# Dealing the products of the unit behind each gate unit out among the gate products, in the second layer of a four-layer model on one core

## The chip, the cores and the metric

One core of a Trainium2 chip runs the whole model in one launch. The metric is the device time of one execution in microseconds, and smaller is better. "Time before" is the median of three runs.

## What is computed

The model has four layers over 512 positions of width 1024: an even mixer (convolution and pooling), an odd mixer (a gated linear recurrence), an S5 state-space layer and a windowed attention layer, the last two with MLPs. The change is in the second layer, the odd mixer:

```python
def odd_mixer(h, w_in, conv_w, conv_b, w_rg, b_rg, w_ig, b_ig, lam, w_out):
    p = h @ w_in                                  # 1024 -> 2 x 1536
    xr, gate = jnp.split(p, [W_LRU], axis=-1)     # 12 heads of 128 each
    xc = causal_depthwise_conv(xr, conv_w, conv_b)
    xh = xc.reshape(bsz, t, LRU_HEADS, LRU_HD)
    r = sigmoid(einsum("bthi,hij->bthj", xh, w_rg) + b_rg)
    i = sigmoid(einsum("bthi,hij->bthj", xh, w_ig) + b_ig)
    log_a = -LRU_C * r * softplus(-lam)
    a = exp(log_a)
    bterm = sqrt(-expm1(2.0 * log_a)) * (i * xc)
    hs = associative_scan(a, bterm)               # over the positions
    y = hs * silu(gate)
    return y @ w_out
```

## The kernel before

**Units.** All matrix work is cut into 281 units in a fixed order (`ORDER`). A unit is a block of weights of 128 x 1024, that is eight 128x128 tiles. Products are made in float32 by splitting both operands in an upper part of reduced precision and the rest: wh x xh, wh x xl and wl x xh. So a unit is 24 matmuls of 512 columns on TensorE (PE). The helper `linear` (lines 310 on; its `product` is L315) runs a unit of one output block: it takes a PSUM bank, waits until that bank is free and the weights' upper part is there, runs sixteen matmuls with the upper weights, waits for the lower weights and runs the last eight.

**Weights.** SyncE (SP) loads unit i into one of three RAW buffers (`fetch`, L268) once the lower part of unit i-3 is made. ScalarE (ACT) makes the upper part WH (`high`, L287; it waits for the load and for the end of unit i-3 on PE, since there are three WH buffers), and GpSimd (POOL) the lower part WL (`low`, L291). Each engine has its own queue in program order; `highs(act, end)` and `lows(pool, end)` put in all roundings up to unit end-1 that are not in yet.

**The order of the second layer** is written out by hand (`ODD`): X0 X1 X2 X3 X4 **R0** X5 ... X11 **R1** G0 ... G5 **R2** G6 ... G11 O0 ... O7 Q0 ... Q3. X is a head's share of xr, G a head's share of the gate, R the two gate matrices of four heads, O and Q the output. Unit R has, for each of its four heads, a product for r and one for i (`mm3`, three matmuls each, lines L298 to L300). These use two PSUM banks of their own in turn (`rbanks`); a gate's bank is freed by ACT's sigmoid, which reads it (`act_gates`: L960 for r into GT, L965 for i into IX). The other units take four banks in turn (`banks`). The bank of an X is free when DVE has written the lower half of the convolved head (`split_lo`, L428, Yl), that of a G when DVE has written the lower half of y (L428 too).

**ACT's queue at an R** (`act_odd`): sigmoids of the first two heads; upper half of an earlier head (`split_hi`, L424, Yh); where the unit before was an X, the first tap of its convolution (L944); sigmoids of the other two heads; where the unit before was a G, its SiLU (L948); rounding of the weights of the unit two behind R (`highs(act, IDX[what] + 3)`); another upper half; rounding of the unit three behind; then tanh for four heads (L927), square root for four (L904) and exponentials (L993), two at once.

**DVE behind it:** for each head three operations on these (`lru_input`, L1072 to L1077) and the scan along the positions (L1082), between them the taps of the convolutions (L1016), the scaled outputs of the units (L421), the products of y (L1021) and the lower halves (L428). Behind R2 DVE also makes a block of coefficients for the third layer (`dve_b`, twice L1255, L1256, L1258: two products of a broadcast row and a table in SBUF, and their sum or difference). POOL multiplies the square root with the head (L1093), makes 1 - x of the tanh product (L1110) and adds the halves of the heads (L1105), between its roundings.

The change touches `pe_odd` and `act_odd`, and adds two functions on PE.

Of the kernel before, what the change touches and what calls it, by code (L numbers as in the profile page):

```python
# [32 lines left out]
for _n, _c in VECS:  # L33
# [15 lines left out]
ODD = ("X0 X1 X2 X3 X4 R0 X5 X6 X7 X8 X9 X10 X11 R1 G0 G1 G2 G3 G4 G5 R2 G6 G7 G8 G9 G10 G11 "  # L49
       "O0 O1 O2 O3 O4 O5 O6 O7 Q0 Q1 Q2 Q3").split()  # L50
EVEN = [(x[0], int(x[1:])) for x in EVEN]
ODD = [(x[0], int(x[1:])) for x in ODD]
# [46 lines left out]
class Signals:  # L99
# [12 lines left out]
    def inc(self, name, key, by=1):  # L112
        s = self.sem(name)
        self.count[name] += by
        assert (name, key) not in self.value, (name, key)
        self.value[name, key] = self.count[name]
        return s, by

    def at(self, name, key):
        s = self.sem(name)  # L120
        assert self.known is None or (name, key) in self.known, (name, key)
        return s, self.known[name, key] if self.known else 1
# [20 lines left out]
def program(nc, ctx, known, D):  # L143
# [128 lines left out]
    def highs(act, end):  # L272

        while upto["hi"] < min(end, len(ORDER)):
            high(act, upto["hi"])
            upto["hi"] += 1
# [17 lines left out]
    def weights(i):  # L294
        return WH[:, i % NS, :], WL[:, i % NS, :]
# [6 lines left out]
    def linear(pe, what, xh, xl, chunks, freed_by, ready=None, between={}, first=False):  # L302


        i = IDX[what]
        wh, wl = weights(i)
        b, before = banks.take(what, freed_by)
        if before:
            pe.wait_ge(*at(*before))
        pe.wait_ge(*at("w_hi" if first or not ready else "w_lo", i))  # L310
        chunks = list(chunks)
        ws = {c: slice(n * 128, n * 128 + 128) for n, c in enumerate(chunks)}

        def product(w, x, c, start=False, stop=False):
            return pe.matmul(b[:, :], w[:, ws[c]], x[:, c, :], start=start, stop=stop)  # L315

        for n, c in enumerate(chunks):
            if ready:
                pe.wait_ge(*at("x_hi", (ready, c)))
            product(wh, xh, c, start=n == 0)  # L320
            if first:
                pe.matmul(CB[0][:, 0:128], MEAN[:, :], MEAN[:, :], start=True, stop=True)
                if n:
                    pe.wait_ge(*at("x_lo", (ready, chunks[n - 1])))
                    product(wh, xl, chunks[n - 1])
            elif ready:
                product(wl, xh, c)
            else:
                product(wh, xl, c)
            if n in between:  # L330
                between[n]()
        if first:
            pe.wait_ge(*at("x_lo", (ready, chunks[-1])))
            product(wh, xl, chunks[-1])
        if first or not ready:
            pe.wait_ge(*at("w_lo", i))
        for c in chunks:
            if ready and not first:
                pe.wait_ge(*at("x_lo", (ready, c)))
                last = product(wh, xl, c, stop=c == chunks[-1])  # L340
            else:
                last = product(wl, xh, c, stop=c == chunks[-1])
        last.then_inc(*inc("unit", what))
# [449 lines left out]
    def odd_what(n):  # L793
        return ODD_UNIT[ODD[n][0]](ODD[n][1])

    rbanks = Banks([])
    rbanks.bank = banks.bank

    def pe_odd(pe):
        for _ in range(2):  # L800
            rbanks.queue.append(banks.queue.popleft())
        for n, (kind, c) in enumerate(ODD):
            what = odd_what(n)
            i = IDX[what]
            wh, wl = weights(i)
            if kind in "XG":
                linear(pe, what, P0h, P0l, range(8), ("x_lo", ("xc" if kind == "X" else "y", c)), "odd" if n == 0 else None)
            elif kind == "O":
                if c == 0:
                    banks.queue.extend(rbanks.queue)  # L810
                linear(pe, what, Yh, Yl, range(8), "h", "y" if c == 0 else None)
            elif kind == "R":
                pe.wait_ge(*at("w_lo", i))
                for h in range(4 * c, 4 * c + 4):
                    pe.wait_ge(*at("x_lo", ("xc", h)))
                    for j, r in enumerate("ri"):
                        b, before = rbanks.take((r, h), "evac_a")
                        pe.wait_ge(*at(*before))
                        ws = slice((h % 4) * 256 + 128 * j, (h % 4) * 256 + 128 * j + 128)
                        last = mm3(pe, b[:, :], wh[:, ws], wl[:, ws], Yh[:, h, :], Yl[:, h, :], True, True)  # L820
                        last.then_inc(*inc("unit", what if (h % 4, j) == (3, 1) else (r, h)))
            else:
                if c == 0:
                    for b in CB:
                        banks.add(b, ("turns", (7, 2)))
                elif c > 1:
                    pe_square_sums(pe, (2 * c - 4, 2 * c - 3))
                pe.wait_ge(*at("w_lo", i))
                for j in range(2):
                    b, before = banks.take(("q4", 2 * c + j), "h")  # L830
                    pe.wait_ge(*at(*before))
                    for kc in range(4):
                        if n == len(ODD) - 4 and j == 0:
                            pe.wait_ge(*at("x_lo", ("y", 8 + kc)))
                        ws = slice((4 * j + kc) * 128, (4 * j + kc) * 128 + 128)
                        last = mm3(pe, b[:, :], wh[:, ws], wl[:, ws], Yh[:, 8 + kc, :], Yl[:, 8 + kc, :], kc == 0, kc == 3)
                    last.then_inc(*inc("unit", what if j else ("q4", 2 * c)))
                    if (c, j) == (3, 0):
                        pe_square_sums(pe, (4, 5))
            if (kind, c) == ("X", 0):  # L840
                stat_sums(pe, "odd", pool=rbanks)
            elif (kind, c) == ("X", 1):
                stat_spread(pe, "odd", pool=rbanks)
# [17 lines left out]
    def kind_at(n):  # L861
        return ODD[n][0] if 0 <= n < len(ODD) else ""
# [20 lines left out]
    def pair(r, second):  # L883
        return [4 * r + 2 * second, 4 * r + 2 * second + 1]
# [5 lines left out]
    def act_odd(act):  # L890
        for n in range(len(ODD) + 3):
            for s, i in late(n):
                act_last(act, i, s)
            if n >= len(ODD):
                continue
            kind, c = ODD[n]
            what = odd_what(n)
            for r, d in gates_at(n):
                if d == 1:
                    for h in pair(r, 0) + pair(r, 1):  # L900
                        act.wait_ge(*at("lru_tanh", h))
                        if h > 3:
                            act.wait_ge(*at("lru_r", h - 4))
                        act.activation(lru_s(h), lru_t(h), ACT.Sqrt).then_inc(*inc("lru_sqrt", h))  # L904
                if d in (1, 3):
                    for h in pair(r, d == 3):
                        lru_exp(act, h)
            if kind == "R":
                act_gates(act, pair(c, 0))
                act_parts(act, n - 1)  # L910
                if kind_at(n - 1) == "X":
                    act_first(act, n - 1)
                act_gates(act, pair(c, 1))
                if kind_at(n - 1) == "G":
                    act_first(act, n - 1)
                highs(act, IDX[what] + 3)
                act_parts(act, n)
                highs(act, IDX[what] + 4)
            elif kind_at(n + 1) != "R":
                highs(act, min(IDX[what] + 4, GLU0))  # L920
                act_first(act, n)
            if kind == "R":
                for h in pair(c, 0) + pair(c, 1):
                    act.wait_ge(*at("evac_a", ("r", h)))
                    if h > 3:
                        act.wait_ge(*at("scan", h - 4))
                    act.activation(lru_t(h), GT[:, h % 4, :], ACT.Tanh, scale=SP4[:, 0, h:h + 1]).then_inc(*inc("lru_tanh", h))  # L927
            elif kind_at(n + 1) != "R":
                act_parts(act, n)
            if kind in "OQ":  # L930
                act_last(act, n, 0)
            elif (kind, c) in (("X", 2), ("X", 9), ("G", 5)):

                act.activation(SM[:, 12 + c % 2:13 + c % 2], SM2[:, 0:1], ACT.Sigmoid)
# [1937 lines left out]
```

## Time and profile before

| what | us |
|---|---|
| median of three runs | 1722.12 |
| lowest and highest of the three | 1722.08, 1727.5 |
| the profiled execution, its own time | 1726.02 |
| the profiled execution, its span | 1724.1 |
| second layer from R0 to the last gate unit (timeline) | 363.5 to 493 |

How to read it: the page gives for each engine the time in which it was busy. A matmul's record lasts about 390 ns, but matmuls are pipelined and follow each other in less; the time of one is that of many back to back. Line numbers are those of the kernel. In a timeline row the square brackets hold the idle time of that engine just before the instruction and the instruction that released it; a wait for several things is put down to the one that came last by the profile.

### The profile page before, as it was taken

Reading aid. Unit: us, or ns where it says so; the run is one execution under the profiler, and the core shown is the slowest. Engines: PE = TensorE matmul, PEld = TensorE weight load, DVE = VectorE, ACT = ScalarE, POOL = GpSimd, SP = SyncE. Lnnn points to the kernel's source line nnn. Section 1 sums busy time; section 2 is a strip of 40 time slices with the busy share of each in tenths; the row PEclk is TensorE's granted clock in tenths of the full one; section 3 lists DMA queues with packets and bytes.
Section 4 is the critical chain, followed back from the end, with each engine's and each line's share of the span. In section 5 each row is a group of like instructions: output and inputs, shape, how many; then the busy total and the mean of one; then the engine's idle time right before and its main releaser. Section 6 shows DMA issues by size and latency. Waiting matters only on the chain.

```text
span 1724.1 us, 20954 instructions
## 1 busy us (share of the span) xinstructions
PE 1698.1 (98%) x8056; PEld 1399.4 (81%) x8056; DVE 869.5 (50%) x1250; ACT 763.1 (44%) x1203; POOL 969.2 (56%) x606
## 2 busy tenths in 40 slices
PE   9999999999999999999999999999999999999998
PEld 7888888777778898888888888887678888888887
DVE  3999997757787785522212121485644221212124
ACT  5333335476867763343222223443664332323234
POOL 5858755657678575654444445664556444444464
PEclk9999999999999999999999999999999999999999
DMA  4322323222245234222222222222112222222221
GB/s 168 106 99 86 111 97 123 90 73 95 86 181 195 67 124 134 98 98 98 98 95 94 95 97 98 89 95 98 38 50 99 98 96 94 95 96 97 98 98 61
DMA packets 56258, 172.65 MB, mean 100 GB/s; under 512 B 6496, under 2 KB 14816, under 8 KB 55264
## 3 DMA queue, kind: packets, MB, share of 16 engines
q1 hardware_dynamic: 56160, 171.33, 28.7%
q8 instruction: 64, 1.05, 0.2%
q14 instruction: 34, 0.28, 0.0%
HBM read 165.01 MB, written 6.29 MB: 99 GB/s over the span
## 4 chain that ended last, share of the span: by engine, by line
PE 68%; DVE 6%; ACT 3%; issue 2%; POOL 2%; DMA 1%; SPq 0%; DVEq 0%; ACTq 0%; POOLq 0%
PE B L315 57%; PE B L2439 1%; PE B L2441 1%; PE B L2437 1%; PE B L2314 1%; PE B L2235 1%; PE B L2335 1%; PE B L298 1%; DVE SW L1150 1%; DVE B L1016 1%; PE B L300 1%; PE B L299 1%; PE B L2411 0%; PE B L2405 0%; PE B L2407 0%
## 5 line engine op out<-in xcount | busy, mean ns | idle before, releaser
L291 POOL TENSOR_TENSOR WL<-RAW,WH 128x1024 fp32r<-128x1024 f32 x281 | 681.5, 2427 | 610.0 <-ACT WH L287 609.7
L287 ACT ACTIVATE WH<-RAW 128x1024 fp32r<-128x1024 f32 x281 | 296.7, 1058 | 627.3 <-PE B L315 595.5
L315 PE MATMUL B<-P0h,WH 128*128 128x512 f32 x1096 | 428.6, 391 | 4.1 <-ACT WH L287 2.3
L315 PE MATMUL B<-P0l,WH 128*128 128x512 f32 x1096 | 422.2, 390 | 0.4 <-DVE P0l L432 0.3
L315 PE MATMUL B<-P0h,WL 128*128 128x512 f32 x1096 | 276.4, 389 | 0.0
L315 PEld LDWEIGHTS B<-P0h,WH 128*128 128x128 f32 x1096 | 206.0, 188 | 48.8 <-DVE Yl L428 2.6
L315 PEld LDWEIGHTS B<-P0l,WH 128*128 128x128 f32 x1096 | 206.0, 188 | 43.2 <-DVE P0l L432 1.1
L315 PEld LDWEIGHTS B<-P0h,WL 128*128 128x128 f32 x1096 | 205.7, 188 | 42.8
L439 DVE TENSOR_TENSOR H<-H,B 128x512 f32<-128x512 f32 x88 | 60.2, 686 | 288.2 <-PE B L315 288.1
L315 PE MATMUL B<-P1h,WH 128*128 128x512 f32 x448 | 174.7, 390 | 0.0
L1967 DVE SCALAR_TENSOR_TENSOR TMP<-B,RS 128x512 f32<-128x512 f32 x64 | 44.1, 691 | 258.4 <-PE B L315 244.1
L315 PE MATMUL B<-P1l,WH 128*128 128x512 f32 x448 | 169.8, 389 | 0.0
L611 DVE SCALAR_TENSOR_TENSOR B<-UP,VE,B 128x512 f32<-128x512 f32 x232 | 156.5, 751 | 1.6 <-ACT B L550 1.6
L315 PE MATMUL B<-P1h,WL 128*128 128x512 f32 x448 | 115.2, 389 | 0.0
L315 PEld LDWEIGHTS B<-P1h,WL 128*128 128x128 f32 x448 | 84.1, 188 | 17.5
L315 PEld LDWEIGHTS B<-P1l,WH 128*128 128x128 f32 x448 | 84.1, 188 | 17.4
L315 PEld LDWEIGHTS B<-P1h,WH 128*128 128x128 f32 x448 | 84.1, 188 | 17.4
L368 POOL TENSOR_TENSOR ACC<-ACC,TMP 128x512 f32<-128x512 f32 x54 | 78.1, 1447 | 22.2 <-ACT TMP L359 21.4
L315 PE MATMUL B<-P2h,WH 128*128 128x512 f32 x144 | 56.2, 391 | 0.7 <-ACT P2h L424 0.7
L2298 POOL TENSOR_SCALAR TMP<-TMP,AS 128x256 f32<-128x256 f32 (+1 forms) x64 | 28.7, 468 | 43.8 <-DVE AS L2292 43.8
L432 DVE SCALAR_TENSOR_TENSOR P0l<-H,VE,P0h 128x512 fp32r<-128x512 f32 x40 | 48.5, 1228 | 9.1 <-ACT P0h L424 9.1
L315 PE MATMUL B<-P2l,WH 128*128 128x512 f32 x144 | 52.6, 389 | 0.0
(354 smaller groups left out, 2699.5 us busy)
## 6 DMA issues: line engine op xcount, KB each, us to landing
RAW<-in_w SPq DMA_DIRECT2D x281, 512.0 KB, 3.2
PX<-in_zeros SPq DMA_DIRECT2D x4, 1024.0 KB, 9.8
H<-in_xT SPq DMA_DIRECT2D x8, 256.0 KB, 5.3
U<-u SPq DMA_DIRECT2D x32, 64.0 KB, 2.0
g<-GB SPq DMA_DIRECT2D x8, 256.0 KB, 2.2
GB<-g SPq DMA_DIRECT2D x32, 64.0 KB, 2.0
out<-Q SPq DMA_DIRECT2D x4, 512.0 KB, 3.6
CA<-in_zeros SPq DMA_DIRECT2D x1, 1920.0 KB, 10.0
```

The lines of the kernel that those rows point to most:

```text
L287: act.activation(WH[:, i % NS, :], RAW[:, i % NR, :], ACT.Copy).then_inc(*inc("w_hi", i))
L291: pool.tensor_tensor(WL[:, i % NS, :], RAW[:, i % NR, :], WH[:, i % NS, :].bitcast(F32), ALU.subtract).then_inc(*inc("w_lo", i))
L298: pe.matmul(out, wh, xh, start=start, stop=False)
L299: pe.matmul(out, wl, xh, start=False, stop=False)
L300: return pe.matmul(out, wh, xl, start=False, stop=stop)
L315: return pe.matmul(b[:, :], w[:, ws[c]], x[:, c, :], start=start, stop=stop)
L368: pool.tensor_tensor(ACC[:, :], ACC[:, :], tmp(c % 2), ALU.add).then_inc(*inc("acc", (k, c)))
L432: dve.scalar_tensor_tensor(dst, src, g, hi.bitcast(F32), ALU.mult, ALU.subtract).then_inc(*inc("x_lo", (k, c)))
L439: dve.tensor_tensor(H[:, n, :], H[:, n, :], banks.bank[what][:, :], ALU.add).then_inc(*inc("h", key))
L611: dve.scalar_tensor_tensor(chunk(c) if j == 30 else CB[c % 2][:, :], UP[:, c, j:j + T], w, CB[c % 2][:, :], ALU.mult, ALU.add).then_inc(*i ...
L1967: dve.scalar_tensor_tensor(mlp_tmp(q, c), banks.bank[what][:, :], 0.0, rs(f"mlp{l}"), ALU.max, ALU.mult).then_inc(*inc("evac_d", what))
L2298: pool.tensor_scalar(s_head(n, h), s_head(n, h), st[:, 16 + h:17 + h], 1.0, ALU.mult, ALU.mult).then_inc(*inc("att_w", (n, h)))
```

## The change

On PE a unit X or G that directly follows an R is no longer run by `linear`. Its 24 matmuls come from a generator, `pe_beside`: the same matmuls in the same order with the same waits on the bank, the upper and the lower weights. `pe_odd` takes two of them after each of the eight gate products of R (sixteen in all) and the last eight behind the last gate. The units concerned are X5 behind R0, G0 behind R1 and G6 behind R2. On ACT, the rounding of the weights of the unit two behind R moves from behind the sigmoids to the front of R's part of the queue.

```diff
--- before.py
+++ after.py
@@ -796,6 +796,29 @@
     rbanks = Banks([])
     rbanks.bank = banks.bank
 
+    def pe_beside(pe, what, freed_by):
+
+        i = IDX[what]
+        wh, wl = weights(i)
+        b, before = banks.take(what, freed_by)
+        pe.wait_ge(*at(*before))
+        pe.wait_ge(*at("w_hi", i))
+        for c in range(8):
+            ws = slice(128 * c, 128 * c + 128)
+            pe.matmul(b[:, :], wh[:, ws], P0h[:, c, :], start=c == 0, stop=False)
+            yield
+            pe.matmul(b[:, :], wh[:, ws], P0l[:, c, :], start=False, stop=False)
+            yield
+        pe.wait_ge(*at("w_lo", i))
+        for c in range(8):
+            last = pe.matmul(b[:, :], wl[:, 128 * c:128 * c + 128], P0h[:, c, :], start=False, stop=c == 7)
+            if c == 7:
+                last.then_inc(*inc("unit", what))
+            yield
+
+    def odd_bank_free(kind, c):
+        return "x_lo", ("xc" if kind == "X" else "y", c)
+
     def pe_odd(pe):
         for _ in range(2):
             rbanks.queue.append(banks.queue.popleft())
@@ -803,14 +826,17 @@
             what = odd_what(n)
             i = IDX[what]
             wh, wl = weights(i)
-            if kind in "XG":
-                linear(pe, what, P0h, P0l, range(8), ("x_lo", ("xc" if kind == "X" else "y", c)), "odd" if n == 0 else None)
+            if kind in "XG" and kind_at(n - 1) == "R":
+                pass
+            elif kind in "XG":
+                linear(pe, what, P0h, P0l, range(8), odd_bank_free(kind, c), "odd" if n == 0 else None)
             elif kind == "O":
                 if c == 0:
                     banks.queue.extend(rbanks.queue)
                 linear(pe, what, Yh, Yl, range(8), "h", "y" if c == 0 else None)
             elif kind == "R":
                 pe.wait_ge(*at("w_lo", i))
+                beside = pe_beside(pe, odd_what(n + 1), odd_bank_free(*ODD[n + 1]))
                 for h in range(4 * c, 4 * c + 4):
                     pe.wait_ge(*at("x_lo", ("xc", h)))
                     for j, r in enumerate("ri"):
@@ -819,6 +845,10 @@
                         ws = slice((h % 4) * 256 + 128 * j, (h % 4) * 256 + 128 * j + 128)
                         last = mm3(pe, b[:, :], wh[:, ws], wl[:, ws], Yh[:, h, :], Yl[:, h, :], True, True)
                         last.then_inc(*inc("unit", what if (h % 4, j) == (3, 1) else (r, h)))
+                        for _ in range(2):
+                            next(beside)
+                for _ in beside:
+                    pass
             else:
                 if c == 0:
                     for b in CB:
@@ -906,6 +936,7 @@
                     for h in pair(r, d == 3):
                         lru_exp(act, h)
             if kind == "R":
+                highs(act, IDX[what] + 3)
                 act_gates(act, pair(c, 0))
                 act_parts(act, n - 1)
                 if kind_at(n - 1) == "X":
@@ -913,7 +944,6 @@
                 act_gates(act, pair(c, 1))
                 if kind_at(n - 1) == "G":
                     act_first(act, n - 1)
-                highs(act, IDX[what] + 3)
                 act_parts(act, n)
                 highs(act, IDX[what] + 4)
             elif kind_at(n + 1) != "R":
```

## Rows read from the trace of the kernel before

**Rows 1.** The page, part 1: busy time of each engine.

```profile
PE 1698.1 (98%) x8056; PEld 1399.4 (81%) x8056; DVE 869.5 (50%) x1250; ACT 763.1 (44%) x1203; POOL 969.2 (56%) x606
```

**Rows 2.** Busy time by stretch: us, busy (instructions) per engine, clock, DMA share, GB/s.

```profile
363.50:371.00 7.50, 6.30 (x26) 4.32 (x25) 5.70 (x8) 5.63 (x9) 0.07 (x1) 1.00 0.19 65
...
409.80:419.30 9.50, 6.26 (x26) 4.28 (x25) 7.96 (x12) 7.08 (x12) 3.62 (x2) 1.00 0.18 55
419.30:451.90 32.60, 32.60 (x145) 27.02 (x144) 21.51 (x31) 28.43 (x38) 27.82 (x18) 1.00 0.29 101
451.90:458.70 6.80, 6.26 (x25) 4.23 (x24) 1.99 (x3) 5.22 (x9) 0.00 (x0) 1.00 0.14 57
```

**Rows 3.** The chain that ended last: start, us, what.

```profile
347.31 16.36 PE B L315 x72
```

**Rows 4.** Timeline, PE and ACT, around R0: start, us, engine, line, operation [idle <-releaser].

```profile
363.52 0.39 PE L298 MATMUL B<-Yh,WH 128*128 128x512 f32 x1
...
364.40 0.69 ACT L960 ACTIVATE GT<-B,VE 128x512 f32<-128x512 f32 x1 [2.49 <-PE B L300]
...
365.23 0.47 PE L298 MATMUL B<-Yh,WH 128*128 128x512 f32 x1 [0.19 <-ACT GT L960]
...
371.15 0.69 ACT L965 ACTIVATE IX<-B,VE 128x512 f32<-128x512 f32 x1
...
371.74 1.05 ACT L287 ACTIVATE WH<-RAW 128x1024 fp32r<-128x1024 f32 x1
...
372.68 0.59 ACT L424 ACTIVATE Yh<-B 128x512 fp32r<-128x512 f32 x1
```

**Rows 5.** Timeline, DVE and PE: what releases X11 and G10.

```profile
403.50 0.68 DVE L428 TENSOR_TENSOR Yl<-B,Yh 128x512 fp32r<-128x512 f32 x1
...
404.23 0.50 PE L315 MATMUL B<-P0h,WH 128*128 128x512 f32 x1 [0.48 <-DVE Yl L428]
...
481.96 0.50 PE L315 MATMUL B<-P0h,WH 128*128 128x512 f32 x1 [1.31 <-DVE Yl L428]
```

**Rows 6.** Timeline, ACT, PE and DVE, at and behind R1.

```profile
412.10 0.68 ACT L960 ACTIVATE GT<-B,VE 128x512 f32<-128x512 f32 x1
...
412.92 0.47 PE L298 MATMUL B<-Yh,WH 128*128 128x512 f32 x1 [1.58 <-DVE Yl L428]
...
419.49 0.69 ACT L965 ACTIVATE IX<-B,VE 128x512 f32<-128x512 f32 x1
...
438.71 0.67 DVE L428 TENSOR_TENSOR Yl<-B,Yh 128x512 fp32r<-128x512 f32 x1
```

**Rows 7.** Timeline, ACT, at and behind R2.

```profile
451.89 0.20 ACT L934 ACTIVATE SM<-SM 128x1 f32<-128x1 f32 x1
...
458.92 0.69 ACT L965 ACTIVATE IX<-B,VE 128x512 f32<-128x512 f32 x1
...
461.41 1.06 ACT L287 ACTIVATE WH<-RAW 128x1024 fp32r<-128x1024 f32 x1
...
462.36 0.59 ACT L424 ACTIVATE Yh<-B 128x512 fp32r<-128x512 f32 x1
...
463.78 2.56 ACT L927 ACTIVATE TMP<-GT,SP 128x512 f32<-128x512 f32 x4
```

**Rows 8.** Timeline, POOL, DVE and ACT, between R2 and G10.

```profile
462.54 5.22 POOL L291 TENSOR_TENSOR WL<-RAW,WH 128x1024 fp32r<-128x1024 f32 x2 [12.24 <-ACT WH L287]
...
463.59 1.92 DVE L1255 TENSOR_TENSOR TMP<-SW,SPT 128x512 f32<-128x512 f32 x1
...
465.43 2.88 DVE L1256 TENSOR_TENSOR ACC<-SW,SPT 128x512 f32<-128x512 f32 x1
...
469.17 1.58 DVE L1255 TENSOR_TENSOR TMP<-SW,SPT 128x512 f32<-128x512 f32 x1
...
471.16 1.30 ACT L993 ACTIVATE B<-GT,SP 128x512 f32<-128x512 f32 x2
...
473.70 0.68 DVE L1072 SCALAR_TENSOR_TENSOR TMP<-B,TMP 128x512 f32<-128x512 f32 x1
```

## The prediction

> **What bounds the kernel now.** The page first: TensorE (PE) is busy for 98% of the span [rows 1], so one would say that any idle PE time is worth its length. The busy time by stage says where PE idles near the change. R0, R1 and R2 are the three stretches of 7.5, 9.5 and 6.8 us in which only 24 products run [rows 2]. One product costs 16.36/72 = 0.227 us where PE runs freely [rows 3], so 24 need 5.45 us, and the three units lose 2.05 + 4.05 + 1.35 = 7.45 us. TensorE's clock is 1.00 throughout [rows 2], its upper level, so the clock plays no part.
>
> The timeline shows why. A gate's sigmoid starts 0.88 us after its first matmul (363.52 to 364.40), takes 0.69, and the matmul that needs the bank starts 0.14 later, at 365.23 [rows 4]. That is 1.71 us for a bank, and with two banks PE asks for it again after 2 x 3 x 0.227 = 1.36.
>
> Then the question that decides: what is late after the gates? ScalarE (ACT) goes from the last sigmoid to the tanh of the four heads, and at the end of that recurrence chain VectorE (DVE) writes the lower halves that free PE's other banks. X11 starts at 404.23, released by the lower half that ended at 403.50 + 0.68 = 404.18; G10 starts at 481.96 after 1.31 idle, also released by a lower half [rows 5]. Between R1 and R2 PE is the bound: 32.60 busy of 32.60 us [rows 2]. So PE is not the only bound: R0 and R2 are each followed by a chain that PE waits for in the end.
>
> **The change.** No product, rounding or DMA is added. Each R and the unit behind it become one run of 48 products, 10.9 us: gate (3), two of the unit behind, gate, and so on, then the unit's last 8. A gate now comes every 5 x 0.227 = 1.135 us and a bank is wanted again after 2.27 us, more than 1.71: PE waits no more where ACT is free. But the last gate product ends later after R's start than an unstalled R would give. And one weight rounding (0.95 from its start to the next instruction, [rows 4]) is moved ahead of the sigmoids in ACT's queue. All sigmoids, and PE through its banks, stand behind it. It waits for the end of the unit before R, which is there as R starts; its RAW slot was filled long before, as the weights' DMA runs on the lower part of the unit three earlier. On GpSimd (POOL) the lower part then comes earlier, and SP's next load too; nobody waits for these now, so I cost both at nothing. The bank and weight waits of the unit behind, now inside the gates, are over before: its weights were rounded during the units ahead and its bank has four units' time.
>
> **R0.** The rounding takes ACT from 363.7 to 364.7, so the first sigmoid is 0.3 late; the next gate comes 1.135 later, so this costs PE nothing. The last gate's first matmul is at 363.5 + 7 x 1.135 = 371.5, and 0.1 more because ACT also works for X3 and X4 between the heads. Its sigmoid starts at 372.5, where it was 371.15: 1.35 later. Behind it ACT no longer has the 0.95 rounding, so tanh and all that follows come 1.35 - 0.95 later: **chain +0.4**. PE finishes R0 and X5 at 363.5 + 10.9 + 0.15 = 374.55, where it was 371.0 + 5.45 = 376.45: **PE -1.9**. But X11 waits for the chain: it starts at 404.23 + 0.4, R1 at 410.2 and not 409.8. R0's gain is gone before R1, and 0.4 with it.
>
> **R1.** Before, ACT's first sigmoid came late, at 412.10, and the third gate product waited for it until 412.92 (1.58 idle; its own first matmul was released by ACT's evacuation, whatever name the row gives) [rows 6]. Now: 412.10 + 0.4 + 0.95 = 413.45, so the third product starts at 413.45 + 0.69 + 0.14 = 414.3. This wait is not removed; it is 1.35 later. Five gates on, with 0.2 for restarts, the last one starts at 420.2 and its sigmoid at 421.1 (before 419.49). Less 0.95: **chain +0.7**. PE ends R1 and G0 at 420.2 + 5 x 0.227 + 8 x 0.227 = 423.2, before 419.3 + 5.45 = 424.75: **PE -1.55**. G4 takes the bank that G0's lower half frees, at 439.38 before [rows 6] and 440.1 now, while PE would be there at 423.2 + 3 x 5.45 = 439.55. G4 starts at 440.15 (before 441.1), R2 at 451.05 (before 451.9): PE -0.9.
>
> **R2.** ACT is free at 452.09 [rows 7], with +0.7 at 452.8, and now rounds first: the first sigmoid is at 453.7, the third product at 454.55, the last at 460.2, its sigmoid at 461.1, where it was 458.92. Here the moved rounding gives nearly nothing back: it stood at 461.41 in the wait for the SiLU's product, which DVE writes, and Yh followed at 462.36 only some 0.1 us after it could [rows 7]. So Yh, DVE behind it and tanh come at **chain +2.1** (tanh 465.9, before 463.78). PE ends R2 and G6 at 463.2 (before 464.15).
>
> **Up to G10.** Does the +2.1 arrive? Before, the two exponentials started at 471.16 and the first ended near 471.8, but DVE took it only at 473.70, because the block of coefficients (L1255, L1256, L1258, twice) stood in front (from 463.59, 9.5 us) [rows 8]. So there are 1.85 us of slack if that block gets shorter. Its price depends on POOL: the first sum's product took 2.88 us beside POOL's two roundings (462.54 for 5.22), a later one of the same kind as the first 1.58 [rows 8], and a plain 128x512 operation of DVE 0.68 [rows 5]. The change takes one of the two roundings away from there. Both ends: the block keeps 9.5 us, then +2.1; or its four products cost 0.7 each, then it ends by 470 and DVE waits for the exponential, at 471.84 + 2.1 = 473.95, which is +0.25. I take the second: it holds once the block takes less than 7.6 us, so 1.9 of 9.5 must go, and two of its products probably lose their partner on POOL (1.92 to 0.7 and 1.58 to 0.7 make 2.1).
>
> DVE waits here on a lock, by the Trainium skill (SBUF — State Buffer, "SBUF: two separate sides"): a DVE operation with two SBUF inputs and a GpSimd one that reads SBUF exclude each other for a whole instruction. The trace agrees: the 2.88 us product ends at 468.31, 0.55 after POOL's rounding at 467.76. By that rule the sum is the same +0.3, and a block of full length would need POOL to win the lock each time.
>
> **Sum.** G10 starts at 481.96 + 0.3 and PE is the bound behind it for the eight O units; the later stages start from there. Total +0.3 us. The profiled execution took 1726.02 (span 1724.1), 3.9 above the median of 1722.12; I add the difference to the median: **1722.4 us**. A floor comes from G9: its weights are rounded behind the exponentials, ready at 471.16 + 1.30 + 1.05 + 2.1 = 475.6 [rows 4, 8], so PE can't reach G10 before 481.0: -0.95.
>
> **Rivals.**
> Slower: the coefficient block keeps its length, and R2's +2.1 goes whole into G10: 1724.2. For: the block ended with POOL's multiplications, which also come 2.1 later. Against: the slack above. It decides once the block takes over 7.6 us. Chance 0.22. A loss over 0.3% (5.2 us, about what a measurement of this kernel can tell from no change) needs all that R's last sigmoids lose, 1.35 + 1.6 + 2.2, unabsorbed: 0.06 with the spread of runs.
> Faster, in full: PE is the bound and its holes are filled, 7.45 + 0.48 at X11 + 1.31 at G10 = 9.2 us: 1712.9. The Trainium skill leans this way (Perfetto Trace Analysis, "Optimization Strategy"): it reads a repeated gap as too few buffers and advises interleaving regimes. Against: 0.48 and 1.31 are waits for DVE, and the holes in R1 are ACT's lateness. Chance 0.06.
> Faster, in part: the chain after R2 has slack that I don't see, and the 0.95 of PE, or some of R1's, survives: -1 to -3.5, 1720. Chance 0.09.
> It doesn't do what it says: the unit behind isn't ready and its products hold the gates. Against: no product of these stretches waits for weights. It would cost about what is gained, 1723. Chance 0.03. Forecast 0.60.
>
> Cases of no change dominate: faster 0.07, same 0.87, slower 0.06. The range reaches down to the partial gain, 1718.5, and up to +2.1 with the upper of the three runs shown (1727.5): 1727.0.
>
> **What would show it.** After: R0 with X5 in 11.0 us, R1 with G0 near 13.0, R2 with G6 near 12.1; a wait of over 1 us at the third gate product of R1 and of R2, released by ACT; X11, G4 and G10 released by DVE's Yl; tanh after R2 near 465.9; G10 near 482.3. I am wrong if G10 starts before 481 or after 484.5, or if the last gates' sigmoids are not later after R's start than now.

## The result, and the profile after

The changed kernel took 1727.66 us (median of 8 runs, 1725.98 to 1728.48) where the kernel before took 1723.16 in the same comparison (8 runs, 1722.08 to 1727.5). The ratio is 1.0024, with a 95% interval from 1.0014 to 1.0033: slower, by less than the 0.3% named above, but by more than its own interval. The time lies 0.66 us above the range of the prediction. In two later comparisons, on two chips, the same two programs differed by 1.0 us (ratio 1.0010, 1.0001 to 1.0018) and by 2.8 us (1.0016, 1.0007 to 1.0025). So two questions stand: what the change itself costs, and why one pair of programs gives three differences.

The profiled execution after has a span of 1725.7 us and its own time is 1727.64. First, TensorE's timeline at the places of [rows 4] to [rows 6]: R0's first matmul, the releases of X9 and X11, R1's third gate product, G4, R2's third gate product, G9 and G10.

```profile
364.16 0.39 PE L298 MATMUL B<-Yh,WH 128*128 128x512 f32 x1
...
393.19 0.50 PE L315 MATMUL B<-P0h,WH 128*128 128x512 f32 x1 [1.46 <-DVE Yl L428]
...
405.29 0.50 PE L315 MATMUL B<-P0h,WH 128*128 128x512 f32 x1 [0.86 <-DVE Yl L428]
...
414.92 0.47 PE L298 MATMUL B<-Yh,WH 128*128 128x512 f32 x1 [1.63 <-ACT GT L990]
...
440.71 0.50 PE L315 MATMUL B<-P0h,WH 128*128 128x512 f32 x1 [0.45 <-DVE Yl L428]
...
455.01 0.47 PE L298 MATMUL B<-Yh,WH 128*128 128x512 f32 x1 [0.82 <-ACT GT L990]
...
476.24 0.47 PE L315 MATMUL B<-P0h,WH 128*128 128x512 f32 x1 [1.48 <-ACT WH L287]
...
483.50 0.50 PE L315 MATMUL B<-P0h,WH 128*128 128x512 f32 x1 [1.53 <-DVE Yl L428]
```

R0 itself now starts 0.64 us later than before (364.16, [rows 4] 363.52), so what follows is counted from R0's first matmul. Every hole that the change fills comes back as a wait: inside R0 TensorE loses nothing any more except 0.2 us, but X9 and X11 wait for VectorE (1.46 and 0.86), R1 and R2 wait for ScalarE at their third product, G4 waits, G9 waits for its weights, and G10 starts 483.50 - 364.16 = 119.34 us behind R0. Before it was 481.96 - 363.52 = 118.44 [rows 4, 5]. The change made this stretch **0.9 us longer**. ScalarE's timeline shows where the time is lost (last sigmoid of R0; R1: rounding, first and last sigmoid; R2: rounding, first and last sigmoid, Yh, tanh):

```profile
373.17 0.69 ACT L995 ACTIVATE IX<-B,VE 128x512 f32<-128x512 f32 x1 [0.47 <-PE B L300]
...
413.15 1.05 ACT L287 ACTIVATE WH<-RAW 128x1024 fp32r<-128x1024 f32 x1
414.10 0.68 ACT L990 ACTIVATE GT<-B,VE 128x512 f32<-128x512 f32 x1
...
421.72 0.69 ACT L995 ACTIVATE IX<-B,VE 128x512 f32<-128x512 f32 x1 [0.44 <-PE B L300]
...
453.25 1.04 ACT L287 ACTIVATE WH<-RAW 128x1024 fp32r<-128x1024 f32 x1
454.20 0.67 ACT L990 ACTIVATE GT<-B,VE 128x512 f32<-128x512 f32 x1
...
461.65 0.69 ACT L995 ACTIVATE IX<-B,VE 128x512 f32<-128x512 f32 x1 [0.44 <-PE B L300]
...
465.00 0.60 ACT L424 ACTIVATE Yh<-B 128x512 fp32r<-128x512 f32 x1 [0.77 <-DVE B L1051]
...
466.45 1.94 ACT L957 ACTIVATE TMP<-GT,SP 128x512 f32<-128x512 f32 x3
```

From R0, the last sigmoids stand at 9.01, 57.56 and 97.49 us; before they stood at 7.63, 55.97 and 95.40 [rows 4, 6, 7]. ScalarE now idles 0.44 to 0.47 us before each of them, released by TensorE: the gates come too far apart for it. VectorE and GpSimd between R2 and G10, against [rows 8] (first VectorE, the coefficient block and what follows it; then GpSimd):

```profile
466.24 0.68 DVE L1285 TENSOR_TENSOR TMP<-SW,SPT 128x512 f32<-128x512 f32 x1
466.84 2.91 DVE L1286 TENSOR_TENSOR ACC<-SW,SPT 128x512 f32<-128x512 f32 x1
469.78 0.69 DVE L1288 TENSOR_TENSOR BB<-TMP,ACC 128x512 f32<-128x512 f32 x1
470.61 0.69 DVE L1285 TENSOR_TENSOR TMP<-SW,SPT 128x512 f32<-128x512 f32 x1
471.22 1.79 DVE L1286 TENSOR_TENSOR ACC<-SW,SPT 128x512 f32<-128x512 f32 x1
473.04 1.67 DVE L1288 TENSOR_TENSOR BB<-TMP,ACC 128x512 f32<-128x512 f32 x1
474.64 0.69 DVE L421 TENSOR_TENSOR B<-B,RS 128x512 f32<-128x512 f32 x1
475.24 0.68 DVE L1102 SCALAR_TENSOR_TENSOR TMP<-B,TMP 128x512 f32<-128x512 f32 x1
```

```profile
466.62 2.57 POOL L291 TENSOR_TENSOR WL<-RAW,WH 128x1024 fp32r<-128x1024 f32 x1 [9.87 <-ACT WH L287]
471.02 3.15 POOL L1123 TENSOR_TENSOR TMP<-TMP,XC 128x512 f32<-128x512 f32 x2 [1.82 <-ACT TMP L934]
```

The block runs from 466.24 to 474.64, 8.4 us, where it took 9.5. Two of its products fell to 0.68 and 0.69. The first (1.92 before) lost its partner, one of GpSimd's two roundings, which is gone from there. The second (1.58 before) lay under the first of GpSimd's multiplications and now ends ahead of it. But the sum at its end, 0.69 elsewhere, took 1.67: it lies under the second multiplication. The multiplications begin as far behind the block's start as before, 4.8 us (471.02 - 466.24 and 468.36 - 463.59 [rows 8]), while the block's earlier operations got shorter. Before, the block's last sum was free (GpSimd and VectorE, kernel before):

```profile
468.36 3.54 POOL L1093 TENSOR_TENSOR TMP<-TMP,XC 128x512 f32<-128x512 f32 x2 [0.60 <-ACT TMP L904]
...
472.49 0.69 DVE L1258 TENSOR_TENSOR BB<-TMP,ACC 128x512 f32<-128x512 f32 x1
```

The rest of the difference is TensorE's clock. In the windows of the profile after, the granted clock was 0.79 from 340 to 348 us, ahead of the changed code, which can't have caused it, and 0.79 and 0.86 at two more places. In the profile before, 340 to 348 us ran at 1.00, and a stretch near 8 us was at the lower level instead. So both profiled executions hold three such stretches, and they differ by only 1.62 us (1727.64 and 1726.02): 0.9 from the change and 0.64 from where R0 starts. Rows of 340 to 348, 548 to 556 and 1196 to 1208 us, first before, then after (the clock is the third number from the end):

```profile
340.00:348.00 8.00, 7.72 (x40) 6.60 (x41) 0.16 (x1) 1.74 (x3) 3.55 (x4) 1.00 0.32 121
548.00:556.00 8.00, 8.00 (x37) 6.70 (x37) 6.63 (x7) 5.74 (x12) 8.00 (x9) 0.79 1.00 419
1196.00:1208.00 12.00, 10.52 (x47) 7.27 (x46) 6.86 (x14) 6.31 (x22) 5.58 (x9) 0.86 0.12 44
```

```profile
340.00:348.00 8.00, 8.00 (x33) 6.57 (x33) 0.16 (x1) 0.38 (x1) 3.22 (x2) 0.79 0.21 75
548.00:556.00 8.00, 7.71 (x35) 6.26 (x34) 6.32 (x6) 5.81 (x12) 8.00 (x10) 0.79 1.01 418
1196.00:1208.00 12.00, 10.51 (x49) 6.89 (x48) 8.21 (x16) 6.18 (x20) 5.59 (x9) 0.86 0.13 44
```

TensorE's timeline after, ahead of the first stretch and inside it:

```profile
339.34 1.02 PE L386 MATMUL B<-MEAN,ACC 128*128 128x1 f32 x8 [0.71 <-POOL ACC L368]
...
340.81 0.63 PE L315 MATMUL B<-P0h,WH 128*128 128x512 f32 x1
341.24 0.63 PE L315 MATMUL B<-P0l,WH 128*128 128x512 f32 x1
...
343.80 0.55 PE L315 MATMUL B<-P0l,WH 128*128 128x512 f32 x1
344.19 0.39 PE L315 MATMUL B<-P0h,WH 128*128 128x512 f32 x1
```

The products follow each other in 0.43 us instead of 0.227, the lower of the two clock levels (1.2 GHz), and eight of them cost 8 x 0.2 = 1.6 us. Ahead of it TensorE had waited 0.71 us for the statistics of the norm and run eight matmuls of one column. The kernel before has the same wait and the same narrow matmuls there, and its clock stayed at 1.00:

```profile
340.28 1.02 PE L386 MATMUL B<-MEAN,ACC 128*128 128x1 f32 x8 [0.71 <-POOL ACC L368]
```

The other two places are alike in that narrow matmuls and a wait interrupt the wide products: sixteen matmuls of two columns for the square sums near 550 us, four 128x128 transposes of attention weights behind a wait of 1.44 us near 1200 us.

### The profile page after: what moved, and what is told of

The parts are those of the page before. It is cut to its first block, busy times and chain, and to the rows that moved or that the text cites. A ratio compares the mean times of both kernels' runs of the same rounds, so it can differ in the third digit from the quotient of the medians.

```text
span 1725.7 us, 20954 instructions
## 1 busy us (share of the span) xinstructions
PE 1698.3 (98%) x8056; PEld 1400.0 (81%) x8056; DVE 868.1 (50%) x1250; ACT 762.9 (44%) x1203; POOL 969.1 (56%) x606
## 3 DMA queue, kind: packets, MB, share of 16 engines
q8 instruction: 64, 1.05, 0.3%
## 4 chain that ended last, share of the span: by engine, by line
PE 67%; DVE 5%; POOL 4%; issue 3%; ACT 3%; DMA 0%; SPq 0%; DVEq 0%; ACTq 0%; POOLq 0%
PE B L315 55%; POOL WL L291 1%; PE B L2469 1%; PE B L2471 1%; PE B L2467 1%; PE B L2344 1%; PE B L2265 1%; PE B L2365 1%; PE B L298 1%; DVE SW L1180 1%; PE B L300 1%; PE B L299 1%; PE B L2441 0%; PE B L2435 0%; PE B L2437 0%
## 5 line engine op out<-in xcount | busy, mean ns | idle before, releaser
L315 PE MATMUL B<-P0h,WH 128*128 128x512 f32 x1072 | 420.0, 392 | 7.0 <-DVE Yl L428 4.3
L315 PE MATMUL B<-P0l,WH 128*128 128x512 f32 x1072 | 413.6, 391 | 1.4 <-DVE P0l L432 1.3
L315 PE MATMUL B<-P0h,WL 128*128 128x512 f32 x1072 | 270.5, 389 | 0.0
L315 PEld LDWEIGHTS B<-P0h,WH 128*128 128x128 f32 x1072 | 201.8, 188 | 52.3 <-DVE Yl L428 6.1
L315 PEld LDWEIGHTS B<-P0l,WH 128*128 128x128 f32 x1072 | 201.8, 188 | 43.5 <-DVE P0l L432 2.3
L315 PEld LDWEIGHTS B<-P0h,WL 128*128 128x128 f32 x1072 | 201.2, 188 | 41.9
```

## The experiments

The theory after the result has two parts. The chain: the gates' new spacing makes the last sigmoid of each R later, and the recurrence chain behind R2 carries that to the gate unit G10. The clock: the rest is the number of stretches at the lower clock. In the expectations, theory A is that this number is chance or hangs on when the later stages begin, theory B that all of the loss is the change's own. Eleven kernels ran, in three groups of one chip each; a comparison was made with 11 or 12 runs of each kernel and about 30 of the kernel before.

| kernel | O units begin, us from R0 | lowest us | median minus before | ratio, 95% interval | low-clock stretches in its profile near |
|---|---|---|---|---|---|
| before (first profile; lowest of all its runs) | 129.46 | 1721.82 | | | 550, 1200 |
| e1 before again | 129.49 | 1722.12 | -0.1 | 0.9999, 0.9990 to 1.0008 | 340 |
| e2 changed again | 130.40 | 1722.89 | +1.0 | 1.0010, 1.0001 to 1.0018 | 340, 550 |
| e3 TensorE's part | 131.74 | 1724.43 | +2.3 | 1.0017, 1.0008 to 1.0025 | 394 |
| e4 ScalarE's part | 128.26 | 1721.38 | -1.05 | 0.9997, 0.9989 to 1.0006 | 340, 550 |
| e5 delay of 0.91 us | 129.49 (+0.91 behind) | 1724.63 | +2.7 | 1.0018, 1.0009 to 1.0027 | 550, 1200 |
| e6 R0 and R1 only | 129.28 | 1722.00 | +0.3 | 1.0004, 0.9995 to 1.0012 | 550, 1200 |
| e7 one product a gate | 129.20 | 1722.12 | -0.3 | 1.0001, 0.9992 to 1.0010 | 416 |
| e8 changed, third | 130.44 | 1722.94 | +2.8 | 1.0016, 1.0007 to 1.0025 | none |
| e9 R2 only | 130.04 | 1722.39 | +0.3 | 1.0002, 0.9994 to 1.0011 | 340, 550, 1200 |
| e10 ScalarE's part again | 128.28 | 1721.64 | -1.2 | 0.9996, 0.9987 to 1.0004 | 340, 550 |
| e11 delay of 1.81 us | 129.46 (+1.81 behind) | 1725.39 | +3.25 | 1.0016, 1.0008 to 1.0025 | 550, 1200 |

The short stretch at the very end of the run, in all profiles, and one at 8 us in the first profile of before are left out of the last column. The stretches of e3 and e7 near 394 and 416 us lie between R0 and the O units, that is inside the span of the first column.

**The same programs again (e1, e2, e8).** No edit.

> The kernel before, unchanged, as an experiment. The profile after the change shows two things: G10 starts 1.54 us later, of which +0.65 was there before R0 (-0.93 from the start of the run, +1.58 from one more stretch at TensorE's lower clock near 340 us), so the change itself made +0.89; and the medians differ by 4.5 us. Theory A (chain and chance): the change costs about 1 us and the rest is the number of low-clock stretches, each worth about 1.6 us. Then this run differs from the kernel before by -2 to +2 us although it is the same program, and its stretches at the lower clock differ in number or place from the first profile's (there at 8, 550, 1200 and 1720 us). Theory B (all of the 4.5 us is the change's): this run agrees with the kernel before within 1 us, and so does its trace.

> The changed kernel again, beside the kernel before. Theory A: +1 to +4 us against the kernel before, and the trace again has G10 0.9 us later counted from R0's start than the kernel before has (119.3 us after R0's first matmul, before 118.4). Theory B: +4 to +5 us and a trace in which the late part lies behind R0.

> The changed kernel a third time, on the chip of this batch. Both theories: G10 at 119.3 us from R0's first matmul. Theory A: 0.5 to 2.5 us above the kernel before and within 1 us of the pure delay of 0.9 us. Theory B: 2 us or more above the kernel before and 1.2 or more above the pure delay.

The kernel before against itself gave 0.9999, which fits both theories; that its profile has one stretch (340 us) where the first had three (8, 550, 1200) is what theory A said. Its lowest runs lie at 1721.8 to 1722.2, others near 1723.6 and 1725.3: steps of 1.6 to 1.7 us. The changed kernel's G10 stood at 119.38 and 119.43 us from R0 in its other two profiles, so the 0.9 us belong to the program. The changed kernel's three profiled executions tell the price of a stretch without any comparison of kernels: 1722.94 us with none of them, 1726.13 with two, 1727.64 with three. That is 3.19/2 = 1.60 and 4.70/3 = 1.57 us each. A stretch near 8 us, which only the first profile of the kernel before has, was cheaper: R0 starts at 363.52 there and at 362.5 to 362.9 in the profiles with no stretch ahead of it. The third profile of the changed kernel, over the same stretches:

```profile
340.00:348.00 8.00, 8.00 (x40) 6.68 (x40) 0.43 (x2) 1.55 (x2) 4.06 (x3) 1.00 0.22 78
548.00:556.00 8.00, 8.00 (x48) 7.04 (x49) 7.27 (x8) 5.75 (x12) 8.00 (x9) 1.00 1.00 423
1196.00:1208.00 12.00, 11.14 (x64) 7.66 (x65) 7.97 (x17) 7.37 (x23) 5.62 (x9) 1.00 0.13 44
```

The program is the one of the first profile after; the clock differs, with it how much work falls into the same windows, and the whole execution is 4.7 us shorter. The lowest runs differ by 1722.89 - 1721.82 = 1.07 us, next to the +0.9 of the timelines. Of e2's expectation theory A held; e8 lay at +2.8, 0.3 above what A had given, and 0.06 from the pure delay.

**The change's two parts (e3, e4, e10).** e3 has only TensorE's part, e4 and e10 only ScalarE's:

```diff
 e3, against the changed kernel
             if kind == "R":
-                highs(act, IDX[what] + 3)
                 act_gates(act, pair(c, 0))
...
                     act_first(act, n - 1)
+                highs(act, IDX[what] + 3)
                 act_parts(act, n)
 e4 and e10, against the kernel before
             if kind == "R":
+                highs(act, IDX[what] + 3)
                 act_gates(act, pair(c, 0))
...
                     act_first(act, n - 1)
-                highs(act, IDX[what] + 3)
                 act_parts(act, n)
```

> Only TensorE's part of the change: ACT rounds the weights of the unit two behind R after the sigmoids, as before. Chain theory: the last sigmoids of R0 and R1 are as late as in the changed kernel but nothing is saved behind them, POOL's two roundings fall into the coefficient block again, so G10 is 2.0 to 2.5 us later from R0 than in the kernel before, more than the changed kernel's 0.9. Rival (the moved rounding does the harm, because it stands ahead of the sigmoids): G10 earlier than in the changed kernel, at or below the kernel before.

> Only ACT's part of the change: the gates run one behind another on TensorE as before, the rounding stands ahead of them. Chain theory: the wait for ACT in R1 gets no longer than 0.3 us more, each chain starts about 0.6 us earlier behind R0 and R1, so G10 comes 0.3 to 1.0 us earlier from R0's start than in the kernel before. Rival (the moved rounding does the harm): G10 0.5 to 1.0 us later than in the kernel before.

> Only ACT's part, again, to see whether its 1.2 us from R0 to the O units (128.26 against 129.46) reach the time. If only the length counts: 1.2 us below the kernel before, ratio 0.9993. If the low-clock stretches follow the start of the later stages in another way for each kernel: anything from -2.5 to +1 us, in steps of 1.6.

Dealing out the products alone costs 131.74 - 129.46 = 2.3 us up to the O units, and moving the rounding alone gains 1.2. So the change is a harmful part and a useful one, 2.3 - 1.2 = 1.1, near the 0.9 measured together. G10 came 2.28 us later in e3, as the chain theory had it (2.0 to 2.5). The rival, that the moved rounding does the harm, falls: e3 leaves it where it was and is worse. The low-clock stretch of e3's profile hides in waits: X11 no longer waits, R1's third product still waits 0.29 us and starts 50.76 us from R0 as in the changed kernel, and R1's last sigmoid is 0.2 us later than there (57.76), so at most that much of the 2.3 can be the stretch's. In e3 the coefficient block is back at full length, as both of GpSimd's roundings lie in it again (VectorE, and G10's release):

```profile
465.11 1.90 DVE L1285 TENSOR_TENSOR TMP<-SW,SPT 128x512 f32<-128x512 f32 x1
466.93 2.89 DVE L1286 TENSOR_TENSOR ACC<-SW,SPT 128x512 f32<-128x512 f32 x1
...
470.68 1.57 DVE L1285 TENSOR_TENSOR TMP<-SW,SPT 128x512 f32<-128x512 f32 x1
472.17 1.78 DVE L1286 TENSOR_TENSOR ACC<-SW,SPT 128x512 f32<-128x512 f32 x1
```

```profile
483.46 0.50 PE L315 MATMUL B<-P0h,WH 128*128 128x512 f32 x1 [2.65 <-DVE Yl L428]
```

G10 waits 2.65 us there. In e4 this wait is gone: from R2's gates on no wide product of the G units waits. Two parts of e4's expectation failed. G10 came 1.2 us earlier, more than the 0.3 to 1.0 expected. And R1's third product waited 2.35 us, 0.8 longer than before, not 0.3: the time saved behind R0 brought TensorE to R1 earlier, and ScalarE did not come earlier with its rounding ahead. Nor is the gain that of chains that start earlier, as expected: R2's last sigmoid is where it was (95.39 and 95.40 us from R0). It is the coefficient block, which got shorter with one rounding less on GpSimd beside it (VectorE in e4):

```profile
464.17 0.68 DVE L1255 TENSOR_TENSOR TMP<-SW,SPT 128x512 f32<-128x512 f32 x1
464.77 2.91 DVE L1256 TENSOR_TENSOR ACC<-SW,SPT 128x512 f32<-128x512 f32 x1
467.71 0.69 DVE L1258 TENSOR_TENSOR BB<-TMP,ACC 128x512 f32<-128x512 f32 x1
468.53 0.69 DVE L1255 TENSOR_TENSOR TMP<-SW,SPT 128x512 f32<-128x512 f32 x1
469.14 1.79 DVE L1256 TENSOR_TENSOR ACC<-SW,SPT 128x512 f32<-128x512 f32 x1
470.97 1.66 DVE L1258 TENSOR_TENSOR BB<-TMP,ACC 128x512 f32<-128x512 f32 x1
```

The gain in the medians is -1.05 and -1.2 us, in 22 runs, as e10 expected if only the length counts, but both intervals hold 1.

**Which R (e6, e9).** The change at R0 and R1 only, and at R2 only; the other units and ScalarE's order there as before:

```diff
-            if kind in "XG" and kind_at(n - 1) == "R":
+            if kind in "XG" and kind_at(n - 1) == "R" and ODD[n - 1][1] in BESIDE:
...
+                if c in BESIDE:
+                    highs(act, IDX[what] + 3)
                 act_gates(act, pair(c, 0))
...
+                highs(act, IDX[what] + 3)
                 act_parts(act, n)
```

with `BESIDE` (0, 1) in e6 and (2,) in e9, and no products dealt out elsewhere.

> The change at R0 and R1 alone; R2 and G6, and ACT's order there, as in the kernel before. Chain theory: R2 starts about 0.8 us earlier from R0 than before, but ACT comes 0.65 us later to its first sigmoid, so the last sigmoid of R2 is where it was (95.4 us from R0's first matmul, within 0.3) and G10 too (118.4, within 0.4): the 0.9 us of the whole change are all R2's. Rival (the losses of R0 and R1 reach G10): G10 at 119.0 or later.

> The change at R2 alone; R0 and R1 on TensorE and ACT as in the kernel before. The chain theory as the runs have it: R2's last sigmoid stands 10.0 us behind R2's start where it was 7.0, R2 starts at 88.4 us from R0 as before, and ACT's rounding ahead of the sigmoids delays the third product by 0.3. So the last sigmoid is at 98.2 to 98.6, the O units start at 130.7 to 131.3 from R0's first matmul (before 129.5, whole change 130.4), more than with the whole change, since R0 and R1 gave R2 0.8 us. Rival (the +0.9 is the sum of small losses at all three): O units at 129.8 or earlier.

e6 came out as expected: last sigmoid of R2 at 95.22 us from R0 (before 95.40), G10 at 118.27, O units 0.2 us early. The idle 6 us that were filled in R0 and R1, with ScalarE's order there, are worth 0.2. e9 met neither text, as its O units at 130.04 lie between the two: the last sigmoid is at 97.21, not 98.2 or more, because a product now comes only every 1.135 us and the rounding ahead of the sigmoids hid in that. R2 alone costs 0.58 us. 0.58 - 0.18 = 0.4 is not 0.9: R0 and R1 bring TensorE to R2 0.8 us early but ScalarE 0.6 late, so that R2's third product then waits 0.82 us for ScalarE (455.01 above). In e9 it doesn't wait, and R2's last sigmoid is 0.3 us earlier than in the changed kernel (97.21 against 97.49).

**The spacing (e7).** One product of the unit behind after each gate instead of two:

```diff
-                        for _ in range(2):
-                            next(beside)
+                        next(beside)
```

> One product of the unit behind after each gate product, where the change takes two; the rounding stays ahead of the sigmoids. A gate now comes every 4 x 0.227 = 0.91 us, over half of the 1.71 us of a bank. Chain theory (the spacing of the gates is what costs): R2's last sigmoid comes at 95 to 96 us from R0's first matmul where the changed kernel has it at 97.5, the coefficient block loses its partner rounding as in the changed kernel, and G10 starts at 117.5 to 118.2, before that of the kernel before (118.4). Rival (the moved rounding costs): G10 at 119 or later as in the changed kernel.

G10 starts at 118.17 us from R0, 1.2 earlier than in the changed kernel and 0.3 before the kernel before, at the late end of what was expected. R2's last sigmoid is at 96.34, later than the 95 to 96 expected: its third gate product waited 0.49 us for ScalarE. So the spacing is what costs, and the kernel is level with the one before. But e4, with the same order on ScalarE and nothing dealt out, is better still by 129.20 - 128.26 = 0.94 us. No run shows a gain from dealing out; how much of the 0.94 belongs to the low-clock stretch among R1's gates in e7's profile is open.

**All positions together.** us from R0's first matmul, read from the profiles; the block is the coefficient block behind R2:

| kernel | R2's last sigmoid | later than before | block takes | G10 | later than before |
|---|---|---|---|---|---|
| before | 95.40 | | 9.5 | 118.44 | |
| e6 R0 and R1 only | 95.22 | -0.18 | 9.5 | 118.27 | -0.17 |
| e3 TensorE's part | 97.70 | +2.30 | 9.5 | 120.72 | +2.28 |
| changed (first profile) | 97.49 | +2.09 | 8.4 | 119.34 | +0.90 |
| e9 R2 only | 97.21 | +1.81 | 8.4 | 119.02 | +0.58 |
| e7 one product a gate | 96.34 | +0.94 | 8.4 | 118.17 | -0.27 |
| e4 ScalarE's part | 95.39 | -0.01 | 8.4 | 117.23 | -1.21 |

G10 comes as much later as R2's last sigmoid does, less 1.2 us where the rounding at R2 was moved: 1.1 of it is the shorter block. In these seven kernels, what happened at R0 and R1 enters only as far as it moves R2's last sigmoid.

**A pure delay (e5, e11).** The kernel before, with k = 4 or 8 products repeated where TensorE is the bound:

```diff
+            if what == ("out_odd", 0, 1) and n == 0:
+                for _ in range(k):
+                    product(wh, xh, c, start=True, stop=True)
             product(wh, xh, c, start=n == 0)
```

> The kernel before with four products of 128x512 repeated at the head of the second O unit, where TensorE is the bound: 4 x 0.227 = 0.91 us of pure delay, the size of what the change does to G10, and nothing else changed. Theory A (the change is a delay of 0.9 us, and how many stretches at the lower clock follow is chance or depends on when the later stages begin): this kernel is 0.5 to 2 us above the kernel before, like the changed kernel on this chip (+1.0 in its last comparison), and its single times stand in steps of about 1.65 us. Theory B (the change brings low-clock stretches of its own through the way TensorE works in R0 to R2): this kernel is 0.9 us above, the changed kernel 2 us or more above.

> The kernel before with eight repeated products in the second O unit: 1.81 us of pure delay, twice that of the earlier one, which came out at +2.7 and not +0.9. If the surplus comes from when the later stages begin (theory A): the surplus is another one here, the median is +1.2 to +4.5, not twice 2.7. If a delay costs three times itself: +5.4.

0.91 us of extra work gave +2.7 us, more than the 0.5 to 2 that theory A had expected, but just what the changed kernel gave on the same chip (+2.8), with R0 to R2 as before. 1.81 us gave +3.25, within what e11 expected. So the surplus over the length, 1.8 and 1.4 us, does not need the change, and does not double with the delay; the 0.4 between the two is within the intervals.

The granted clock of each run, its mean over the span, sorts the runs by how much of them ran at the lower level. Medians at equal clock over the later comparisons, the kernel before in us and the others as the difference to it, with the number of runs (those of the changed kernel include the eight of the first comparison; e5 has one more, at 0.995):

| granted clock | before | changed | e4 and e10 | e5, delay of 0.91 | e11, delay of 1.81 |
|---|---|---|---|---|---|
| 0.999 | 1722.11 (29) | +0.83 (3) | none | none | none |
| 0.998 | 1723.65 (39) | +0.98 (7) | -1.20 (13) | +1.03 (2) | +1.88 (4) |
| 0.997 | 1725.25 (17) | +1.06 (9) | -1.26 (8) | +1.02 (7) | +1.87 (4) |
| 0.996 | 1726.36 (10) | +1.45 (11) | -1.01 (1) | +1.73 (1) | +2.21 (3) |

At equal clock each kernel costs about its length in the timeline: the change 0.8 to 1.1 us in the upper three rows, the delays 1.0 and 1.9, ScalarE's part -1.2. In the last row the runs of the kernel before alone lie up to 1.5 us apart. The rest of each difference of medians is how many runs stand in which row. e3 and e7 are left out: the profiled execution of each, with a stretch at a place where TensorE waits anyway, is the lowest of its eleven runs. In the first comparison all eight runs of the changed kernel stand at 0.996 or 0.997, in e2 eight of eleven at 0.998 or 0.999: that is the +4.5 and the +1.0.

Of the kernel before 29 of 95 runs stand at 0.999, of the changed kernel 3 of 30, of the two delays none of 22, and none of 22 of e4 and e10, whose later stages begin earlier. So a shift of about 1 us, either way, goes with another number of stretches. By what rule was not tried, and why the changed kernel's runs fell so differently in the first comparison and in e2 stays open.

## Why the prediction was wrong

**The bound, and each R: right.** Counted from R0, prediction and profile: last sigmoid of R0 9.0 and 9.01; X11 41.1 and 41.13; R1's third product 50.8 and 50.76; its last sigmoid 57.6 and 57.56; G4 76.63 and 76.55; R2 87.53 and 87.60; its third product 91.03 and 90.85; its last sigmoid 97.6 and 97.49; tanh 102.4 and 102.29; G9's weights 112.1 and 112.08. The gain of 1.9 us behind R0 was taken back at X9 and X11, most of it at X9, which the text didn't name.

**"I take the second" in "Up to G10": the term of the sum that was mis-sized.** The coefficient block was to fall under 7.6 us, so that VectorE waits for the exponential: +0.25. It took 8.4 us. Both products that were to lose their partner did, 1.92 to 0.68 and 1.58 to 0.69. What failed is that the rest was held constant. GpSimd's multiplications keep their distance to the block's start, so as the block's first operations get shorter, its last sum moves under the second multiplication (0.69 to 1.67). e4 has the same six durations within 0.01 us, although R2's chain is not late there. The step was to save 2.1 us and saved 1.1, and R2's +2.1 arrives as +0.9, between the two ends of that step, 0.25 and 2.1. The clause in the slower rival, that the block ended with the multiplications, was the right one, at less than half the price that it was given.

The exclusion that the prediction cited from the Trainium skill (SBUF — State Buffer, "SBUF: two separate sides") holds here to the row: the block's last sum ends at 474.71, 0.54 after GpSimd's second multiplication at 474.17. Applied to each operation with GpSimd's measured times it gives the length of all six; I used it to confirm a number, not to work one out.

**"TensorE's clock is 1.00 throughout ... so the clock plays no part", and "I add the difference to the median": the step that put the time out of the range.** The clock was looked up only around the change. Elsewhere, the three profiled executions of the changed kernel contain none, two and three stretches at the lower level, 1.6 us each, and the changed kernel's runs hold more of them than those of the kernel before. The sum added the difference to a median of mostly undisturbed runs, 1722.12. The change costs about 1 us at equal clock, but 2.7 us in the median over all 30 runs of the changed kernel and 103 of the kernel before (1726.32 and 1723.64), and 4.5 us in the comparison of the result. The range's upper end doesn't hold what it was said to hold, +2.1 and the upper of the three runs: at 1727.0 it lies below that run alone (1727.5). The forecast of no change beyond 0.3% held (0.24%), in part by luck: the difference was +4.5 us in that comparison, not +0.3.

**The rivals.** Full gain: fell, G10 and X11 do wait for the chain. Partial gain: not in the change; ScalarE's part alone gained 1.2 us up to the O units and at equal clock, by a shorter block and not by filled holes. That the unit behind is not ready: fell, no gate waits for weights. Slower: right in sign, for R2's delay does reach G10, by 0.9 of its 2.1 us.

## What to carry to other kernels

Filling an engine's holes pays only if nothing waits for the work between the holes. Look at the last result of the interrupted work, here the last gate's sigmoid: spread out over 10 us instead of 7 it came 2.1 us later, and a chain of ScalarE, VectorE and GpSimd hung on it. If it must be filled, fill sparingly: one product a gate instead of two took the loss back, and none at all was still better. And split a change into its parts before judging it: this one held a move that gained 1.2 us and one that lost 2.3. The gain came from an unlooked-for place: a rounding moved on ScalarE took its partner on GpSimd away from VectorE.

If a kernel's runs stand in steps, compare runs of equal granted clock and positions inside the timeline, and read the clock over the whole span, not only at the change. The lowest runs alone can mislead: e5's lowest is 2.8 us above that of the kernel before, for a delay of 0.91.

## What the runs showed of the hardware

A stretch at the lower clock cost 1.57 to 1.60 us in the changed kernel's profiles. In most profiles it came at one of three places (340, 550, 1200 us), after narrow matmuls or waits. In e3 it came near 394 us behind a wait of 2.39 us at X9, in e7 near 416 us behind one of 2.05 us at R1's third product; e4 waited 2.35 us at that product, and its clock stayed at 1.00. Repeating four products (0.91 us) in the second O unit moved the median by 2.7 us, 1.0 of it at equal clock. In e3 the stretch cost at most 0.2 us: its profiled execution, which had it, was the lowest of that kernel's eleven (1724.43), for TensorE was ahead of the chain there and lost only waits.

A VectorE operation on two inputs in SBUF was, in all rows read here, either free or held up whole: it took 0.68 to 0.70 us alone, or ended 0.5 to 0.6 us after the GpSimd operation beside it.
